# Differential attention: the joining of two softmaxes shared between the vector engine and GpSimd by halves of the keys, with transposes and values interleaved on PE

## What is computed

```python
# q, k: [tokens, 4 heads, 2, 32]; v: [tokens, 4 heads, 64]; query blocks of 128
s = einsum('bqhmd,bkhmd->bhmqk', q_blk, k) * scale + bias[None, :, None]
p = softmax(s, axis=-1)
w = p[:, :, 0] - lam * p[:, :, 1]
out = einsum('bhqk,bkhe->bqhe', w, v)
# then an RMS norm over the 64 values of each head
```

## Time and profile before

| | |
|---|---|
| median of 3 runs | 2862.53 us (2861.84 to 2866.97) |
| profiled execution, its own time | 2857.84 us |
| its span | 2856.1 us |
| PE busy over the span | 2708.1 us (95%) |
| vector engine (DVE) busy | 1553.1 us (54%) |
| ACT busy | 988.6 us (35%) |
| GpSimd (POOL) busy | 315.0 us (11%) |
| mean granted TensorE clock | 0.978 |
| DMA, HBM read and written | 198.24 MB, 43.05 MB |
| stage of the 32 attention steps, first score product to last join | about 1861.6 to 2008.9 us |

### The profile page before, as it was taken

The page is one execution under the profiler, slowest core; times in us unless marked ns, Lnnn a source line. Parts: engine busy times, 40 slices in busy tenths (PEclk is TensorE's granted clock), DMA queues, the critical chain, the costliest instruction groups (busy, mean ns, idle before and its releaser), DMA issues. The chain is left out here.

```text
span 2856.1 us, 38316 instructions
## 1 busy us (share of the span) xinstructions
PE 2708.1 (95%) x15464; PEld 2247.5 (79%) x15464; DVE 1553.1 (54%) x2456; ACT 988.6 (35%) x1836; POOL 315.0 (11%) x273
## 2 busy tenths in 40 slices
PE   5999999999889999999988989988999999999998
PEld 3789888878766798888887778855688888888886
DVE  4312575777644512766766545879744444444445
ACT  3201233665522401235645334278522211211112
POOL 0000100331331001101314400000100000000001
PEclk8999999999999999999989999999999999999999
DMA  7222222116455413331154431100400110110111
GB/s 271 96 87 80 78 74 89 26 31 223 147 186 186 145 58 90 86 93 48 38 193 129 148 117 46 39 15 1 155 1 30 60 59 29 59 59 29 59 47 78
DMA packets 135894, 248.67 MB, mean 87 GB/s; under 512 B 27106, under 2 KB 90260, under 8 KB 127936
## 3 DMA queue, kind: packets, MB, share of 16 engines
q1 hardware_dynamic: 114592, 231.83, 24.2%
q10 hardware_dynamic: 21152, 14.75, 1.6%
HBM read 198.24 MB, written 43.05 MB: 84 GB/s over the span
## 5 line engine op out<-in xcount | busy, mean ns | idle before, releaser
L969 PE MATMUL ps<-xn_hi_sb,ft_hi_sb 128*128 128x512 f32 (+1 forms) x720 | 263.1, 365 | 1.0 <-DVE ft_lo_sb L1412 1.0
L970 PE MATMUL ps<-xn_lo_sb,ft_hi_sb 128*128 128x512 f32 (+1 forms) x720 | 262.3, 364 | 0.0
L971 PE MATMUL ps<-xn_hi_sb,ft_lo_sb 128*128 128x512 f32 (+1 forms) x720 | 262.2, 364 | 0.0
L3146 DVE TENSOR_TENSOR arena_sb<-arena_sb,ps 128x512 f32<-128x512 f32 x256 | 172.9, 686 | 121.4 <-PE ps L2829 118.5
L919 PE MATMUL ps<-tm_hi_sb,xn_hi_sb 128*128 128x512 f32 (+2 forms) x608 | 216.3, 356 | 11.4 <-DVE tm_lo_sb L1322 7.8
L921 PE MATMUL ps<-tm_hi_sb,xn_lo_sb 128*128 128x512 f32 (+2 forms) x608 | 213.8, 352 | 0.0
L920 PE MATMUL ps<-tm_lo_sb,xn_hi_sb 128*128 128x512 f32 (+2 forms) x608 | 213.6, 351 | 0.0
L2788 PE MATMUL ps<-xn_hi_sb,w_up_hi_sb 128*128 128x512 f32 x512 | 199.4, 389 | 0.0
L2790 PE MATMUL ps<-xn_hi_sb,w_up_lo_sb 128*128 128x512 f32 x512 | 199.2, 389 | 0.0
L2789 PE MATMUL ps<-xn_lo_sb,w_up_hi_sb 128*128 128x512 f32 x512 | 199.2, 389 | 0.0
L2827 PE MATMUL ps<-w_down_hi_sb,h_hi_sb 128*128 128x512 f32 x480 | 186.8, 389 | 0.0
(11 more groups left out here) (422 smaller groups left out, 6115.7 us busy)
## 6 DMA issues: line engine op xcount, KB each, us to landing
arena_sb<-in_w_ft SPq DMA_DIRECT2D x44, 512.0 KB, 3.6
arena_sb<-mqk_dram SPq DMA_DIRECT2D x36, 512.0 KB, 3.4
arena_sb<-x_dram SPq DMA_DIRECT2D x33, 512.0 KB, 6.9
arena_sb<-in_w_ada SPq DMA_DIRECT2D x16, 1024.0 KB, 9.1
arena_sb<-in_w_up SPq DMA_DIRECT2D x16, 1024.0 KB, 6.6
arena_sb<-in_w_down SPq DMA_DIRECT2D x16, 1024.0 KB, 4.8
arena_sb<-in_xall SPq DMA_DIRECT2D x20, 512.0 KB, 5.1
arena_sb<-mv_dram SPq DMA_DIRECT2D x40, 256.0 KB, 3.9
```

Of the source, the lines that this page charges most:

```text
L969: pe.matmul(to, hi, xn_hi_flat[:, k, at:at + size], start=k == 0, stop=False)
L970: pe.matmul(to, hi, xn_lo_flat[:, k, at:at + size], start=False, stop=False)
L971: mm = pe.matmul(to, lo, xn_hi_flat[:, k, at:at + size], start=False, stop=k == KT - 1)
```

## The change

Each join is cut in two. The vector engine joins keys 0 to 511 as before (now L3010). GpSimd does keys 512 to 1023 in two instructions, a multiply of p1 by the factor in place (L3510), then an add to p0 (L3512), both counted on `d_w`, which now rises by three a step. The factor's small operation becomes a `tensor_scalar` on the vector engine (L3005), and the vector engine's join waits for GpSimd's add of the step before. PE transposes in two halves (L2625), each with its own wait, and the values come in quarters (L2637): the first quarter between the two halves of the transposes, the second where the half was. ACT's exponential for m = 0 waits for both halves of the transposes, that for m = 1 now waits for GpSimd's add, and the copy to `w_t` for both halves.

```diff
@@ -2380,8 +2380,9 @@
 
             d_q, d_s, d_nm, d_e = sem("d_q"), [sem(f"d_s{m}") for m in range(2)], [sem(f"d_nm{m}") for m in range(2)], \
                 [sem(f"d_e{m}") for m in range(2)]
+            FIRST_P, REST_P = slice(0, SEQ // 2), slice(SEQ // 2, SEQ)
             d_w, d_t, d_t_act, d_pv, d_y = [sem(n) for n in ("d_w", "d_t", "d_t_act", "d_pv", "d_y")]
-            d_chain = Chain(sem("d_chain"))
+            d_chain, d_ratio = Chain(sem("d_chain")), sem("d_ratio")
             o_square, o_eps, o_var, o_ln, o_rs, o_done = [sem(n) for n in ("o_square", "o_eps", "o_var", "o_ln", "o_rs", "o_done")]
             rep_ld, rep_round, kq_lo_ev, rep_mm, rep_ev, q_mm, kb_ld, kb_ev = [sem(n) for n in ("rep_ld", "rep_round", "kq_lo_ev", "rep_mm", "rep_ev", "q_mm", "kb_ld", "kb_ev")]
 
@@ -2455,7 +2456,7 @@
                 for m in range(2):
                     sp.wait_ge(d_s[m], 4 * NX)
                 sp.dma_start(wo_raw[0], A["w_out2"][0]).then_inc(wo_ld[0], 16)
-                sp.wait_ge(d_t, 4 * NX)
+                sp.wait_ge(d_t, 8 * NX)
                 sp.dma_start(wo_raw[1], A["w_out2"][1]).then_inc(wo_ld[1], 16)
                 for t in range(NX):
                     load_x(t)
@@ -2616,26 +2617,26 @@
                                 mm = pe.matmul(ps[:, 2 * m + c, P * (b % 4):P * (b % 4 + 1)], slope[:, h, :], alibi[:, :], start=False, stop=True)
                         mm.then_inc(d_s[m], 1)
 
-                    def turn_p(s, h):
-                        pe.wait_ge(d_w, s + 1)
-                        if not isinstance(s, int) or s > 0:
+                    def turn_p(s, h, half):
+                        pe.wait_ge(d_w, 3 * s + 2 * half + 1)
+                        if half == 0 and s > 0:
                             pe.wait_ge(d_t_act, s)
-                        for n in range(NX):
-                            mm = pe.transpose(ps[:, 4 + n // 4, (n % 4) * P:(n % 4 + 1) * P], prob2[h % 2][0][:, n * P:(n + 1) * P], ident[:, :])
+                        for n in range(4 * half, 4 * half + 4):
+                            mm = pe.transpose(ps[:, 4 + half, (n % 4) * P:(n % 4 + 1) * P], prob2[h % 2][0][:, n * P:(n + 1) * P], ident[:, :])
                         mm.then_inc(d_t, 1)
 
-                    def values(b, p, half):
-
-                        if half == 0:
+                    def values(b, p, quarter):
+
+                        if quarter == 0:
                             pe.wait_ge(d_t_act, 4 * b + 2 * p + 2)
                             if p == 0 and b > 0:
                                 pe.wait_ge(d_y, b)
-                        for n in range(4 * half, 4 * half + 4):
+                        for n in range(2 * quarter, 2 * quarter + 2):
                             for g in range(2):
                                 at = DH * (2 * p + g)
                                 mm = pe.matmul(ps[DH * g:DH * (g + 1), 6, P * p:P * (p + 1)], v2_tm[:, n, at:at + DH], w_t[p][g][:, n, :],
                                                start=n == 0, stop=n == NX - 1)
-                        if half == 1:
+                        if quarter == 3:
                             mm.then_inc(d_pv, 1)
 
                     def query_block(b, u):
@@ -2647,13 +2648,18 @@
                             more = h < 2 or not last
                             if more:
                                 scores(*following, 0)
-                            turn_p(s, h)
+                            turn_p(s, h, 0)
+                            if h >= 2:
+                                values(b, 0, 2 * h - 4)
+                            elif not first:
+                                values(b - 1, 1, 2 * h)
+                            turn_p(s, h, 1)
                             if more:
                                 scores(*following, 1)
                             if h >= 2:
-                                values(b, 0, h - 2)
+                                values(b, 0, 2 * h - 3)
                             elif not first:
-                                values(b - 1, 1, h)
+                                values(b - 1, 1, 2 * h + 1)
                             if s == 0:
                                 queries(6)
                                 queries(7)
@@ -2673,8 +2679,8 @@
                     for j in range(2):
                         pe.wait_ge(d_e[j], 4 * NX)
                         group_mean(dw_acc, j, mu_mm)
-                    for half in range(2):
-                        values(NX - 1, 1, half)
+                    for quarter in range(4):
+                        values(NX - 1, 1, quarter)
 
                 def group_mean(src, n, done):
                     for c in range(2):
@@ -2989,24 +2995,26 @@
                         dve.tensor_reduce(neg_max[:, u, 2 * h + m:2 * h + m + 1], ps_flat[:, 1024 * m:1024 * (m + 1)], AX_X, ALU.max, negate=True)\
                             .then_inc(d_nm[m], 1)
 
-                    def combine(s, u, h):
+                    def ratio(s, u, h):
 
                         dve.wait_ge(d_e[1], s + 1)
                         dve.wait_ge(d_e[0], s + 1)
-                        ch.start(2 * s)
+                        ch.start(s)
                         c = recip[:, u, 2 * h + 1:2 * h + 2]
                         ch(dve, dve.reciprocal(c, l_all[:, s // 4, 2 * h + 1:2 * h + 2]))
-                        ch(dve, dve.scalar_tensor_tensor(out=row_max[:, u, h:h + 1], in0=l_all[:, s // 4, 2 * h:2 * h + 1], scalar=neg_lam[:, :], in1=c,
-                                                         op0=ALU.mult, op1=ALU.mult))
+                        dve.tensor_scalar(row_max[:, u, h:h + 1], l_all[:, s // 4, 2 * h:2 * h + 1], neg_lam[:, :], c, ALU.mult, ALU.mult).then_inc(d_ratio, 1)
                         p0, p1 = prob2[h % 2]
-                        dve.scalar_tensor_tensor(out=p0, in0=p1, scalar=row_max[:, u, h:h + 1], in1=p0, op0=ALU.mult, op1=ALU.add)\
-                            .then_inc(d_w, 1)
+                        dve.wait_ge(d_ratio, s + 1)
+                        if s > 0:
+                            dve.wait_ge(d_w, 3 * s)
+                        dve.scalar_tensor_tensor(out=p0[:, FIRST_P], in0=p1[:, FIRST_P], scalar=row_max[:, u, h:h + 1], in1=p0[:, FIRST_P],
+                                                 op0=ALU.mult, op1=ALU.add).then_inc(d_w, 1)
 
                     def query_block(b, u):
                         for h in range(4):
                             s = 4 * b + h
                             last = isinstance(b, int) and b == NX - 1
-                            combine(s, u, h)
+                            ratio(s, u, h)
                             if h < 3 or not last:
                                 maximum(s + 1, *((u, h + 1) if h < 3 else (1 - u, 0)), 1)
                             if h < 2 or not last:
@@ -3322,13 +3330,13 @@
 
                     def exp(s, u, h, m):
                         act.wait_ge(d_nm[m], s + 1)
-                        if m == 0 and (not isinstance(s, int) or s >= 2):
-                            act.wait_ge(d_t, s - 1)
+                        if s >= 2:
+                            act.wait_ge((d_t, d_w)[m], (2, 3)[m] * (s - 1))
                         act.activation(prob2[h % 2][m], ps_flat[:, 1024 * m:1024 * (m + 1)], ACT.Exp, bias=neg_max[:, u, 2 * h + m:2 * h + m + 1],
                                        accum_out=l_all[:, s // 4, 2 * h + m:2 * h + m + 1]).then_inc(d_e[m], 1)
 
                     def evacuate(s, h):
-                        act.wait_ge(d_t, s + 1)
+                        act.wait_ge(d_t, 2 * s + 2)
                         act.activation(w_t[h // 2][h % 2].rearrange("p n q -> p (n q)"), ps_flat[:, 2048:3072], ACT.Copy).then_inc(d_t_act, 1)
 
                     def attended(b):
@@ -3494,7 +3502,18 @@
 
                 with pool.Fori(2, NX) as t:
                     root("1", t)
+                def combine(s):
+
+                    h, u = s % 4, s // 4 % 2
+                    p0, p1 = prob2[h % 2]
+                    pool.wait_ge(d_w, 3 * s + 1)
+                    pool.tensor_scalar(p1[:, REST_P], p1[:, REST_P], row_max[:, u, h:h + 1], None, ALU.mult).then_inc(d_w, 1)
+                    pool.wait_ge(d_w, 3 * s + 2)
+                    pool.tensor_tensor(p0[:, REST_P], p0[:, REST_P], p1[:, REST_P], ALU.add).then_inc(d_w, 1)
+
                 spatial_norm()
+                for s in range(4 * NX):
+                    combine(s)
                 for c in range(2):
                     high_wo(c)
                 with pool.Fori(0, NX) as t:
```

## The result

The changed kernel takes 2868.8 us (median of 12 runs, 2865.14 to 2873.41); the kernel before, on the same chip, 2862.59 (12 runs). The ratio is 1.0024, with a 95% interval of 1.0014 to 1.0035: slower by 4 to 10 us. Forecast were 2865.7 us in a range of 2856.5 to 2872.5, +3.2 us.

A forecast was written before the change was run, and what follows sets the result against it. The vector engine bounds the attention's 4.15 us steps, PE nearly those with queries; the bound moves to a ring through ACT and PE. Start -1.0, queries +1.3, eighteen steps +1.0, end +1.9: +3.2, 2865.7 us, range 2856.5 to 2872.5.

The forecast's parts named there:

- the gaps of 0.17: PE's weight loads idle 0.17 us at every crossing between transposes or scores and values; four crossings a step, two before.
- The ring through ACT and PE: Loop of exponential, copy, four transposes, quarter of values, last transposes, back to ACT: 4.20 us a step against 4.15.
- the first rival: PE's gap does not recur in the new order: ring 3.86, sum -5.5 to -7.5, about 2856 us; chance 0.18.
- The multiply on GpSimd: GpSimd's multiply of 512 keys by a column, priced at 0.65 us between bounds 0.61 and 2.6.
- the second rival: GpSimd is late, deciding from a multiply of 1.7 us; at 2.54, steps of 4.57, +14, 2876.5 us; chance 0.14.
- a slack of 1.1 us: GpSimd's lead before PE reaches the second transposes, so a multiply of up to 1.7 us costs nothing.
- the loop through GpSimd: Two-step loop of half join, multiply m, add, transposes, ACT and next join: 6.6+m us.
- The eight steps with queries: Steps that carry a query projection, bound by PE: 5.0 us against 4.85, +1.3 us in all.
- The eighteen steps: Steps 13 to 31, without queries, at the ring's 4.20 us against 4.15: +1.0 us.
- The start: Steps 2 to 5: the vector engine's 3.6 us shows in two steps, 0.5 each: -1.0 us.
- The end: After the last join, GpSimd's last pair and the vector engine's folds take turns: +1.9 us; PE's loss covered, uncovered 3 us.
- The whole 0.55 gone: Third rival: each step's full vector engine saving reaches the end result, -8 us and more, 2854; chance 0.06.

The follow-up runs named there:

- e2: Changed kernel with GpSimd's multiply covering 16 of its 512 keys, the other 496 left unscaled: ratio 1.0011, 4.16 us a step in steps 13 to 31.
- e3: Changed kernel with PE's old order (both transpose halves, second scores, then values), joins still shared: ratio 1.0021, 4.27 us a step in steps 13 to 31.
- e5: Changed kernel with all joins whole on the vector engine, keeping the new PE order and small multiply's new form: ratio 1.0000, 4.26 us a step.
- e4: Changed kernel with GpSimd's multiply over only 16 keys and PE's old order together: ratio 0.9968, 3.73 us a step in steps 13 to 31.
- e1: Changed kernel with only the last step's join whole on the vector engine: ratio 1.0000 to the kernel before, end 10.74 us.
- e10: Changed kernel with the vector engine's folds held until GpSimd's last add is done: ratio 1.0017, end 13.24 us.
- e6: Changed kernel with joins split 768 keys (vector engine) and 256 (GpSimd), PE's old order, last join whole: ratio 0.9971, 3.94 us a step.
- e9: Changed kernel split 640/384 keys, two-input GpSimd multiply, interleaved values only in steps 4 to 11, last join whole: ratio 0.9971, 3.81 us a step.
- e7: Changed kernel with PE's old order and GpSimd's multiply as a two-input operation with the column broadcast: one run, 3.99 us a step, end 15.43.

## Why the prediction was right and where it was off

**The forecast's mechanism held**: a change of bound at nearly the same pace. The limits it named are in the trace: the vector engine with time to spare, ACT's exponentials behind the last transposes, the gaps of 0.17 around the new quarter of values. The sum is off, +3.2 against some +6.3 by stage (1.0 to the last join, 5.3 behind it), which agrees with the measured ratio (1.0024, 6.9 us).

**The ring through ACT and PE: right.** 4.20 forecast, 4.16 with GpSimd out of the way (e2). The gap recurs, which was the doubtful point and the first rival. Weight loads around one quarter of values in the changed kernel, timeline:

```profile
1950.69 0.42 PEld L2637 LDWEIGHTS ps<-arena_sb 128*64 128x64 f32 x8 [0.17 <-issue]
...
1951.28 0.42 PEld L2625 LDWEIGHTS ps<-ident_sb,arena_sb 128*128 128x128 f32 x4 [0.17 <-issue]
```

0.17 in and 0.17 out, where no wait is named. The Trainium skill (TensorEngine Tiling (Array Packing), Key Properties) says that a change of the tiling mode drains the engine, and the trace agrees in the main: from 1875 to 2010 us the gap stands at all 29 crossings from transposes to values and at all 29 back (longer where PE also waits), and the kernel before shows the same 0.17 in and out of its values; only out of the bias product (L2617) into values the loads stand idle 0.06 (16 times).

**The multiply on GpSimd: wrong by 0.92 us.** The step that failed is "I take 0.65, since it too reads one tensor". It takes 1.57 at 512 keys, 0.92 at 256, 0.33 at 16: 0.3 us and 2.5 ns for each key, against 0.61 for a whole cast of 512. It was between the bounds (0.61 and 2.6), and below the 1.7 from which the second rival was to decide. Yet a slack of 1.1 us did not make it free: the loop through GpSimd was written as 6.6+m, 8.17 us or 4.08 a step with m = 1.57, and the lap shown above measured 8.61, the difference being chiefly the copy of the attended block (0.39) that stands on ACT inside it and was not counted. At 4.27 (e3) beside a ring of 4.16 (e2) it decides in part of the steps: the forecast took one limit, and there are two. The price is 0.09 x 18 = 1.6 us.

**The eight steps with queries: the sign was wrong.** Forecast 5.0, measured 4.73, and 4.85 before. Weight loads of one such step:

```profile
1916.42 0.42 PEld L2637 LDWEIGHTS ps<-arena_sb 128*64 128x64 f32 x8 [0.24 <-issue]
1917.01 0.19 PEld L2599 LDWEIGHTS ps<-q_hi_sb,rep_sb 128*128 128x128 f32 x1 [0.17 <-issue]
...
1918.10 0.19 PEld L2614 LDWEIGHTS ps<-k_st_sb,q_st_sb 112*128 112x128 f32 x1 [0.25 <-issue]
...
1919.33 0.42 PEld L2637 LDWEIGHTS ps<-arena_sb 128*64 128x64 f32 x8 [0.17 <-issue]
1919.92 0.42 PEld L2625 LDWEIGHTS ps<-ident_sb,arena_sb 128*128 128x128 f32 x4 [0.17 <-POOL arena_sb L3512]
1920.30 0.19 PEld L2614 LDWEIGHTS ps<-k_st_sb,q_st_sb 112*128 112x128 f32 x1
...
1921.10 0.42 PEld L2637 LDWEIGHTS ps<-arena_sb 128*64 128x64 f32 x8 [0.24 <-issue]
```

From one second quarter to the next, 4.68: 0.59 for the quarter, 1.09 for the query, 1.23 for scores and four transposes (forecast 1.31), 0.59 for the first quarter (0.65), 0.38 for the last transposes (0.5), 0.80 for scores. Four of the six pieces were priced 0.06 to 0.12 too high, and all six together 0.32. The forecast also set this bare sum against a step of 4.85 that held a wait of PE on ACT, and did not ask what the new order does to that wait: it ends it (PE busy 20.00 of 20), because a quarter of values now stands where PE waited. e3, without that quarter, is at 4.97; e5, with the order and whole joins, at 4.66. Measured 8 x -0.12 = -0.9 for the forecast's +1.3.

**The eighteen steps: mechanism right, size off.** +1.8 for +1.0. The ring came out 0.04 a step shorter than forecast and is worth only some 0.2 of it; the other 1.6 are the multiply's part. **The start**: -1.0 was forecast for steps 2 to 5, from two steps at 3.6. They took 4.18 (+0.1): with GpSimd's long multiply the vector engine's 3.6 never shows there; with the short one (e2) they took 3.91, with e4's order 3.73.

**The end: this decided the size.** Forecast +1.9, measured +5.3. The step that failed is "What PE and SyncE lose there ... is covered by the folds, which end later; uncovered it would be 3 us". Nor did the two engines take turns as forecast: each fold ran at its full 1.22, and GpSimd paid for both, so the folds' +1.9 became +0.8 (the last of them ends 10.40 us after the last join, 9.57 before). PE's lateness became what counts, and was priced too low. The last transposes start 5.90 us behind the last join; before, the last four of eight started 1.75 behind it (1.34+0.41). That is 4.15; the clock adds 0.9 on transposes and values and 2.1 on the statistics; eight value products fewer stand behind the transposes (-0.5). PE's last values thus end 15.7 us after the last join, 9.0 before: 6.7 later, less the 1.3 by which the squares waited for the vector engine before, is 5.3. The cover was there, but it was 1.3 us wide. e1 shows that the whole 5.3 hang on this one join. The Trainium skill (SBUF — State Buffer, Who interferes with whom) says that the pair of ports the vector engine and GpSimd share is an exclusive lock, that a vector instruction with two SBUF inputs contends with a GpSimd instruction that reads SBUF, and that issue order decides who blocks. The trace agrees for the first fold, 0.08 us ahead of the multiply, and in e10 for the cast, 0.41 ahead of a fold; it also shows the second fold going ahead of the waiting multiply.

**The rivals.** The gap that doesn't recur: refuted. GpSimd late: not as a step of 4.57, but present, at 4.27 and in part of the steps. The whole 0.55 gone: 0.42 of it comes only with both limits away (e4). The two errors of sign and size in the stage cancel (+1.0 in all against +1.3), so the forecast was near for the stage partly by luck; the end carries the rest.

**Left open.** Why the way from the small multiply to the join is 0.36 us in e5 and 0.31 in the kernels with shared joins, what the old form of that multiply would give in e6 to e9, and why steps 0 to 2 vary so much between executions.

## What to carry to other kernels

When work is moved to an idle engine, write down every loop that the moved piece closes, with all that stands in it (the small copy once in four steps too); two loops at 4.2 hide each other, and only a run without both shows what the move could give. Price an operation by a row of the same form, not of the same number of inputs, and move less than half if the idle engine is the slower: in the same order on PE, 768 and 256 keys ran at 3.94 a step (e6) and 512 and 512 at 4.27 (e3). Look too at the small operations that a change rewrites on the way: the way from the reciprocal to the join grew by 0.06 to 0.11 us a step here. And treat the last step of a pipeline by itself: there nothing is left to cover a late piece, the next stage's work meets it on the shared resource, and an idle PE can lose its clock; here one join of 32 done the old way was worth 5.3 us.

## What was not expected of the hardware

- A multiply by a per-row column on GpSimd took 0.33, 0.92 and 1.57 us at 16, 256 and 512 keys, 2.5 ns for each further key. The same product as a two-tensor multiply with the column broadcast takes 1.04 us at 512 and 0.83 at 384. The two-tensor add takes 0.73, 1.00 and 1.27 us at 256, 384 and 512.
- A GpSimd multiply that came 0.08 us behind the first of two back-to-back two-input vector operations was held through both (3.62 us instead of 1.57), while neither of these was stretched (1.22 us each); e3 has the same 3.62. A two-tensor multiply at that place (e7, one profile) took 2.05 instead of 1.04, and there the second vector operation took 2.06. Later in the change, four vector additions beside a cast took 7.25 us in all.
- The length of one wait does not tell whether PE's clock falls: products stood idle 3.33 us in the change, and PE went on at 1.2 GHz; they stood 1.61 in e5, and it fell to 1.2 only after four more transposes; they stood 1.69 at the same place before and 1.25 in e10, and it went on at 2.4.
